# Delta rule: the row sums of squares in two reduced-precision products, moved later in the tensor engine's order

## The reference

```python
def step(state, inp):
    q_c, k_c, u_c, w_c, g_c, a_c = inp
    v_new = u_c - einsum('bhcd,bhde->bhce', w_c, state)
    o = (einsum('bhcd,bhde->bhce', q_c * exp(g_c)[..., None], state)
         + einsum('bhij,bhje->bhie', a_c, v_new))
    ...
    state = state * exp(g_last)[..., None, None] + einsum('bhcd,bhce->bhde', k_dec, v_new)
    return state, o
...
o = gated_delta_rule(qf, kf, vf, g, beta)
o = o * lax.rsqrt(jnp.mean(o * o, axis=-1, keepdims=True) + EPS) * o_norm_g
o = o * jax.nn.silu(z)
...
h = h + concatenate([y_pool, y_dn], axis=-1) @ w_out
```

## Time and profile before

| | |
|---|---|
| median of three runs | 1951.04 us |
| the profiled execution, its own time | 1952.26 us |
| its span, first to last instruction | 1950.5 us |
| mean granted tensor engine clock | 0.997 of full |
| PE busy | 1936.3 us, 99% of the span |
| VectorE (DVE) busy | 1237.9 us, 63% |
| ScalarE (ACT) busy | 870.2 us, 45% |
| chain that ended last | PE 93%, DVE 4%, ACT 1%, issue 1% |

### The profile page before, as it was taken

The page is one execution under the profiler, slowest core; times in us unless marked ns, Lnnn a source line. Parts: engine busy times, 40 slices in busy tenths (PEclk is TensorE's granted clock), DMA queues, the critical chain, the costliest instruction groups (busy, mean ns, idle before and its releaser), DMA issues.

```text
span 1950.5 us, 26540 instructions
## 1 busy us (share of the span) xinstructions
PE 1936.3 (99%) x10262; PEld 1599.0 (82%) x10262; DVE 1237.9 (63%) x1842; ACT 870.2 (45%) x1308; POOL 13.6 (1%) x31
## 2 busy tenths in 40 slices
PE   9999999999999999999999999999999999999998
PEld 7888888888777888888888888887888888888887
DVE  6667566598998745765545457786665566444534
ACT  6445344433676363543323245842654442222222
POOL 0000000000000000000000000010000000000000
PEclk9999999999999999999999999999999999999999
DMA  7989898454433553444555333551143233323231
GB/s 241 301 290 301 299 287 282 165 190 167 140 121 130 194 188 125 138 164 160 185 169 177 130 112 119 197 183 41 55 144 119 94 100 103 100 90 105 88 107 65
DMA packets 91308, 310.51 MB, mean 159 GB/s; under 512 B 10376, under 2 KB 12808, under 8 KB 91184
## 3 DMA queue, kind: packets, MB, share of 16 engines
q1 hardware_dynamic: 90032, 307.70, 47.1%
q10 hardware_dynamic: 1152, 1.12, 0.2%
HBM read 264.66 MB, written 43.53 MB: 158 GB/s over the span
## 4 chain that ended last, share of the span: by engine, by line
PE 93%; DVE 4%; ACT 1%; issue 1%; DMA 0%; ACTq 0%; POOL 0%; POOLq 0%; DVEq 0%
PE ps L368 27%; PE ps L372 27%; PE ps L369 27%; DVE cacc L2098 1%; PE ps L391 1%; PE ps L392 1%; PE ps L394 1%; PE ps L588 1%; PE ps L736 1%; PE ps L566 0%; PE ps L578 0%; DVE ps L2218 0%; ACT P L1403 0%; PE ps L931 0%; PE ps L934 0%
## 5 line engine op out<-in xcount | busy, mean ns | idle before, releaser
L368 PE MATMUL ps<-Hh,whi 128*128 128x512 f32 x1432 | 560.8, 392 | 1.3 <-DVE vml L2783 1.3
L372 PE MATMUL ps<-Hh,wlo 128*128 128x512 f32 x1432 | 557.6, 389 | 0.0
L369 PE MATMUL ps<-Hl,whi 128*128 128x512 f32 x1432 | 557.4, 389 | 0.0
L1197 ACT CAST whi<-raw 128x1024 fp32r<-128x1024 f32 (+2 forms) x346 | 347.2, 1009 | 355.4 <-PE ps L372 311.9
L1959 DVE TENSOR_TENSOR wlo<-raw,whi 128x1024 fp32r<-128x1024 f32 (+2 forms) x267 | 309.8, 1166 | 152.9 <-ACT whi L1197 147.9
L368 PEld LDWEIGHTS ps<-Hh,whi 128*128 128x128 f32 x1432 | 268.8, 188 | 61.7 <-issue 4.3
L372 PEld LDWEIGHTS ps<-Hh,wlo 128*128 128x128 f32 x1432 | 268.8, 188 | 56.5
L369 PEld LDWEIGHTS ps<-Hl,whi 128*128 128x128 f32 x1432 | 268.9, 188 | 55.0
L2098 DVE SCALAR_TENSOR_TENSOR cacc<-upad,gains,cacc 128x512 f32<-128x512 f32 x232 | 160.2, 745 | 0.7
L2044 DVE SCALAR_TENSOR_TENSOR x<-ps,x 128x512 f32<-128x512 f32 x79 | 54.6, 691 | 145.1 <-PE ps L372 145.1
L2020 DVE TENSOR_TENSOR scr<-ps,Rt 128x512 f32<-128x512 f32 (+1 forms) x100 | 66.7, 667 | 59.5 <-PE ps L372 40.3
(11 more groups left out here) (415 smaller groups left out, 2934.9 us busy)
## 6 DMA issues: line engine op xcount, KB each, us to landing
raw<-in_w SPq DMA_DIRECT2D x388, 512.0 KB, 4.3
low_parts<-lo SPq DMA_DIRECT2D x58, 512.0 KB, 4.3
wlo<-low_parts SPq DMA_DIRECT2D x58, 512.0 KB, 3.3
late_low_parts<-lo SPq DMA_DIRECT2D x21, 512.0 KB, 5.1
wlo<-late_low_parts SPq DMA_DIRECT2D x21, 512.0 KB, 3.4
raw<-in_w SPq DMA_DIRECT2D x16, 384.0 KB, 3.0
raw<-in_w SPq DMA_DIRECT2D x21, 256.0 KB, 2.6
out<-y SPq DMA_DIRECT2D x8, 256.0 KB, 2.1
```

Of the source, the lines that this page charges most:

```text
L368: e.matmul(out, h[:, kk, :], a, start=part != "last" and k + kk == 0, stop=False)
L369: e.matmul(out, h[:, kk, :], c, start=False, stop=False)
L372: ins = e.matmul(out, lo[:, kk, :], a, start=False, stop=done)
L1197: e.copy(whi[i % WS][:, 0:n], raw[i % RAWS][:, 0:n]).then_inc(*act.tick("whi", ("whi", i)))
```

## The change

Three things change. The sums for chunks 1, 2 and 3 are made by `mean_row` from a high part `on_h` (a copy by ScalarE) and a low part `on_l` (a subtraction by VectorE, written over the squares), in place of one fp32 product. There is one buffer for squares instead of two, so `on_square(c)` waits until the sum of chunk c-1 has been made. And the order changes on three engines: PE makes sum 1 behind `kv(2)`, sum 2 behind `o(3)`, and sum 3 where it was; ScalarE makes the squares of chunk 3 and their high part ahead of the inverse root of chunk 2; VectorE makes the new values of chunk 3 ahead of `on_unit(1)`.

```diff
--- before.py
+++ after.py
@@ -225,6 +225,7 @@
         turned_g = (scr[5], scr[2])
         qk_h = [at(f"qk_h{i}", o_vb + 2048 * (1 + i), [128, T], F32R) for i in range(3)]
         qk_l = [at(f"qk_l{i}", SCR + 2048 * (3 + i), [128, T], F32R) for i in range(3)]
+        on_h, on_l = at("on_h", SCR + 2048, [128, T], F32R), at("on_l", SCR, [128, T], F32R)
         pool_h, pool_l = at("pool_h", o_Tm, [128, 4, T], F32R), at("pool_l", o_up, [128, 4, 528], F32R)
 
         blk32 = lambda t: t.rearrange("p (m c) -> p m c", c=32)
@@ -866,7 +867,10 @@
                 gemm(("w2", j), "w_out_2", 4, 4, [(128 * j, 128)], Ydh, Ydl, "yd", part="last")
 
             def on_row(c):
-                full_row(("on", c), "on_sq", c, src=scr[c % 2])
+                if c:
+                    mean_row(("on", c), on_h, on_l, 0)
+                else:
+                    full_row(("on", 0), "on_sq", 0, src=scr[0])
 
             for c in range(4):
                 cur, v_ = St[c % 2], vn[c % 2]
@@ -878,7 +882,8 @@
                     for h in range(4):
                         ins = e.matmul(b[:, 128 * h:128 * h + 128], wT[:, h, c, :], cur[:, h, :], start=True, stop=True)
                     ins.then_inc(*pe.tick("rule", ("wS", c)))
-                    on_row(c - 1)
+                    if c == 1:
+                        on_row(0)
                     if c >= 2:
                         first_half(c - 2)
                     pe.wait_ge("vn", c)
@@ -890,6 +895,8 @@
                     for h in range(4):
                         ins = e.matmul(b[:, 128 * h:128 * h + 128], kdec[:, h, c, :], new(h), start=True, stop=True)
                     ins.then_inc(*pe.tick("rule", ("kv", c)))
+                if c == 2:
+                    on_row(1)
                 o = take(("o", c))
                 for h in range(4):
                     oo = o[:, 128 * h:128 * h + 128]
@@ -899,6 +906,7 @@
                         e.matmul(oo, cur[:, h, :], qkv[:, h, 4 + 128 * c:132 + 128 * c], start=True, stop=False)
                     ins = e.matmul(oo, new(h), aT[:, h, c, :], start=c == 0, stop=True)
                 ins.then_inc(*pe.tick("rule", ("o", c)))
+            on_row(2)
             first_half(2)
             on_row(3)
             first_half(3)
@@ -1745,9 +1753,12 @@
 
             def on_square(c):
                 act.wait_ge("o", c)
-                if c >= 2:
-                    act.wait_ge("spread", ("on", c - 2))
-                e.activation(scr[c % 2][:, :], ps(("o", c))[:, :], AF.Square).then_inc(*act.tick("sq", ("on_sq", c)))
+                if c:
+                    act.wait_ge("spread", ("on", c - 1))
+                e.activation(scr[0][:, :], ps(("o", c))[:, :], AF.Square).then_inc(*act.tick("sq", ("on_sq", c)))
+                if c:
+                    act.wait_ge("on_sq", c)
+                    e.copy(on_h[:, :], scr[0][:, :]).then_inc(*act.tick("row_hi", ("row_hi", ("on", c))))
 
             def on_high(c):
                 root_row(("on", c), 1.0 / 128)
@@ -1760,9 +1771,12 @@
             for c in range(4):
                 if c >= 2:
                     after(("w2", c - 2, "first"))
+                if c == 3:
+                    on_square(3)
                 if c:
                     on_high(c - 1)
-                on_square(c)
+                if c < 3:
+                    on_square(c)
                 if c:
                     yd_high(c - 1)
             after(("w2", 2, "first"))
@@ -2698,6 +2712,11 @@
                 dve.wait_ge("po", g)
                 low(Ypl[:, g, :], scr[(4, 5, 2, 3)[g]][:, :], Yph[:, g, :], "yp", g)
 
+            def on_low(c):
+                dve.wait_ge("on_sq", c)
+                dve.wait_ge("row_hi", ("on", c))
+                e.tensor_tensor(on_l[:, :], scr[0][:, :], on_h[:, :].bitcast(F32), SUB).then_inc(*dve.tick("row_lo", ("row_lo", ("on", c))))
+
             def on_unit(c):
                 s3 = scr[4 + c % 2][:, :].rearrange("p (h c) -> p h c", h=4)
                 sl = slice(128 * c, 128 * c + 128)
@@ -2731,25 +2750,32 @@
                                                      in1=ps(("kv", c))[:, 128 * h:128 * h + 128], op0=MUL, op1=ADD)
                 ins.then_inc(*dve.tick("St", ("St", c + 1), ("free", ("kv", c))))
 
-            new_state(0)
-            pool_low(0)
-            for c in range(1, 4):
+            def new_v(c):
                 dve.wait_ge("wS", c)
                 if c >= 3:
                     dve.wait_ge("o", c - 2)
                 e.tensor_tensor(vn[c % 2][:, :, :], u_[:, :, c, :], ps(("wS", c))[:, :].rearrange("p (h c) -> p h c", h=4), SUB).then_inc(
                     *dve.tick("vn", ("vn", c), ("free", ("wS", c))))
-                if c == 1:
-                    pool_low(1)
-                if c < 3:
-                    new_state(c)
-                if c == 1:
-                    pool_low(2)
-                    pool_low(3)
-                    weights(ends["w2", 0, "first"] + 1)
-                if c >= 2:
-                    after(("w2", c - 2, "first"))
-                on_unit(c - 1)
+
+            new_state(0)
+            pool_low(0)
+            new_v(1)
+            pool_low(1)
+            new_state(1)
+            pool_low(2)
+            pool_low(3)
+            weights(ends["w2", 0, "first"] + 1)
+            on_unit(0)
+            new_v(2)
+            on_low(1)
+            new_state(2)
+            after(("w2", 0, "first"))
+            new_v(3)
+            on_unit(1)
+            on_low(2)
+            after(("w2", 1, "first"))
+            on_low(3)
+            on_unit(2)
             after(("w2", 2, "first"))
             after(("w2", 3, "first"))
             on_unit(3)
```

## The result

| | before | changed |
|---|---|---|
| median, 11 runs each | 1952.67 us | 1957.95 us |
| lowest to highest | 1949.48 to 1955.67 | 1955.16 to 1960.95 |
| span of the profiled execution | 1950.5 us | 1953.5 us |
| its own time | 1952.26 us | 1955.31 us |
| PE busy | 1936.3 us | 1934.9 us |

A forecast was written before the change was run, and what follows sets the result against it. PE, busy 99% of the span, was taken to bound the kernel. Waits net of saved products, 4.0 us, plus 1.1 us of clock on 1951.04 gave 1956.1 us, range 1953.4 to 1958.6.

The forecast's parts named there:

- The sum: Whole kernel: 4.0 us of later second_half(0) plus 1.1 us of clock, added to 1951.04 us, gives 1956.1 us.
- the clock: Gap ahead of first_half(5): granted clock falls to half for about three microseconds, costing 0 to 1.6 us, taken as 1.1.
- What that releases on ACT: ACT after sum 2: later roots delay P+4, P+5 and a bank, PE waits, second_half(0) starts 4.0 us later.
- The products: Sums of three chunks on PE: two products of 0.46 us replace 0.85 us each, about 1.2 us less work.
- Same waits, clock stays up: Rival: the waits cost 4.0 us and the clock does not fall, 1955.0 us; chance 0.28.
- Not slower: Rival: ACT keeps ahead of PE and only the saved products remain, 1950.8 us; chance 0.08.
- A shorter root: Rival: a root on ACT needs one table load, so the change costs 1.4 us, 1952.4 us; chance 0.05.

The follow-up runs named there:

- weights early: Changed kernel with P+4 and P+5 converted ahead of the roots of chunks 2 and 3 on ACT; ratio to the kernel before 1.0014, wS(1) to second_half(0) 32.71 us.
- fp32 sums: Changed kernel's order, but sums of chunks 1 to 3 as single fp32 products again; ratio to the kernel before 1.0031, wS(1) to second_half(0) 34.92 us.
- sum 2 late: Kernel before with only the fp32 sum of chunk 2 moved behind the output of chunk 3 on PE; ratio 1.0012, wS(1) to second_half(0) 32.23 us.

## What held of the prediction, and the step that failed

**Sign and mechanism** came out as forecast: 5.1 us slower predicted, 6.1 measured (4.5 to 7.6). The absolute number did less well. The forecast was 1956.1 us with an upper end of 1958.6. The changed kernel's median is 1957.95, and the ratio on the median before gives 1958.7, just past that end. Two terms of "The sum" were mis-sized, and the first is the larger.

**The step that failed: "this execution lies 1.2 us above the median of the three, which gives 1951.04 + 5.1".** It took a median of three executions for the level of the kernel before. Over eleven executions that median is 1952.67 us, 1.6 us higher, and the profiled execution (1952.26) lies 0.4 us below it and not 1.2 above. The range was laid around this level without any room for its error, so two thirds of the 2.6 us between 1956.1 and 1958.7 were lost before the change was priced.

**The other: the clock, "I take 1.1 us".** It stood for one fall at a reduced price. In the profiled execution the one fall of the stage cost 1.57 us, nearly the upper bound of 1.6. Over all executions 6.1 us less 4.2 us of waits leaves 1.9 us beside them (0.3 to 3.4 by the interval); by the medians it is 5.3 less 4.2, which would be the forecast's 1.1. So something is paid beside the waits, its size in the usual execution is not known well, and that it is the clock is shown for the profiled execution alone. The reasoning behind it was also weaker than it looks. It priced the fall by comparing the new gap of 2.7 us with the old one of 2.1, and left the gap of 1.3 us out as too short. But the old gap at 1338 us was 1.42 us in the kernel with weights early, and a fall followed; it was 1.46 us in the changed kernel, and none followed. So that the fall came behind the gap that was named was in part luck, and whether the shorter gaps matter stays open: filling the last gap alone left the mean clock at 0.9974, and filling all three gave 0.9979, with some ten executions each.

**The waits**, 4.0 us in "What that releases on ACT": 4.16 us in the profile once the fall is taken out, and 34.77 and 34.79 us of length in the two kernels without one, against 34.6 worked out. Term by term: 1.07 us idle ahead of `kv(2)` (1.1 forecast), no wait at any sum (none forecast), then, by the starts as the prediction counts, 1.35 us for P+4's high part (1.3) and 0.31 for its low part (0.35), and 2.54 us ahead of `first_half(5)` (2.7), with the releaser that was named. The bank was the right one; that DVE's chain ends at nearly the same time, so that the bank alone is worth little, was shown by giving it another bank.

**The products**: "about 1.2 us less PE work" was right in size, 1.14 us by the starts. In the change's own order the waits are more than four times that, and taking the products back there changes nothing.

**The rivals.** "Same waits, clock stays up" happens in single executions (the fp32 sums ran through the gap at full clock), but its 4.0 us lie below the interval of 4.5 to 7.6 us. "Not slower" needed P+4's high part at PE in time; it came 1.2 us late. "A shorter root" did not occur: a table load stands ahead of Ln and another ahead of Exp as before, and from the first at 1388.06 the root takes 3.84 us.

## What to carry to other kernels

On a kernel whose tensor engine is busy all the time, follow each moved instruction on the other engines' queues to the next thing that the tensor engine needs from that queue: here the sum moved by 5 us, and the cost came from the weight conversions and a bank release that stood behind its root. Splitting a product into a high and a low part shortens it on one engine and lengthens the way to it by a copy and a subtraction on two others. In this kernel it paid only where the order gave it that time. Where a saving is a thousandth of the run, measure the stretch between two fixed instructions in the trace, since whole runs spread by more than the effect.

## What the runs showed that I had not expected

- The length of a gap did not decide whether the clock fell. 2.39 us was followed by a fall in the changed kernel and by none with fp32 sums. The old gap at 1338 us, which nothing here touches, was 2.11 us before, with a fall, and 1.83 us in two other kernels, with a fall when only the last gap was filled and without one when all three were. Nine of the twelve profiles have a fall there:

```profile
1341.00:1342.00 1.00, 1.00 (x4) 0.71 (x4) 0.97 (x2) 0.00 (x0) 0.00 (x0) 0.50 0.09 16
...
1340.00:1341.00 1.00, 1.00 (x5) 0.83 (x6) 0.95 (x2) 0.00 (x0) 0.00 (x0) 1.00 0.08 16
```

(The first line is of the kernel with the last gap filled, the second of that with all three.) The changed kernel's profile has none there. In two kernels (weights early, sum 2 late) the clock fell at about 1269 us too, with no idle time of PE listed from 1262 to 1285. The changed kernel has no such fall either. So its profiled execution lost one fall at 1338 us and gained one at 1400.
- A fall costs the full price when PE has work for it: twelve products in 4.45 us and not 2.88. Two kernels with the same length without falls can then differ by 1.6 us in a profile.
- Products with a useless result, put into idle time of PE, made the length no longer: with 18 of them the length was 34.79 us, against 34.77 with nine. Whether they make a kernel faster is not settled by these intervals.
